# A group's four squared output tiles added on GpSimd before one product with ones, behind the next projection tile

## The reference, cut to what matters

```python
y = y + p['d_skip'][:, None].astype(y.dtype) * xs
y = y.reshape(b, T, D_INNER) * jax.nn.silu(z)
y = rmsnorm(y.reshape(b, T, N_GROUPS, D_INNER // N_GROUPS),
            p['ssd_norm_w'].reshape(N_GROUPS, D_INNER // N_GROUPS)).reshape(b, T, D_INNER)
merged = jax.nn.sigmoid(ga) * (attn @ p['w_pa']) + jax.nn.sigmoid(gb) * (y @ p['w_pb'])
```

## The kernel before, in words

| group | before | later |
|---|---|---|
| 0 | (z, 1, 0) | (z, 1, 1) |
| 1, 2 | (pb, g - 1, 6), two tiles | (z, g + 1, 0), (z, g + 1, 1) |
| 3 | (pb, 2, 6), two tiles | none |

## Time and profile before

### The profile page before, as it was taken

The page is one execution under the profiler, slowest core; times in us unless marked ns, Lnnn a source line. Parts: engine busy times, 40 slices in busy tenths (PEclk is TensorE's granted clock), DMA queues, the critical chain, the costliest instruction groups (busy, mean ns, idle before and its releaser), DMA issues.

```text
span 1709.2 us, 27847 instructions
## 1 busy us (share of the span) xinstructions
PE 1621.0 (95%) x10961; PEld 1453.3 (85%) x10965; DVE 760.9 (45%) x927; ACT 630.9 (37%) x1009; POOL 374.4 (22%) x417
## 2 busy tenths in 40 slices
PE   4998999999999999999999989899989999999997
PEld 3993336888999898889988988899979999999997
DVE  3444454222225667665766665535233333232221
ACT  4437665333223434523533442323132332332221
POOL 6003334542002444344134234100000000000000
PEclk9998999989999999999999999899979999999999
DMA  3221002433332222222223222253202222223331
GB/s 101 80 69 37 0 1 81 136 116 103 96 110 66 86 82 68 87 81 85 68 78 87 81 75 87 64 148 110 63 25 87 85 75 86 86 74 92 102 91 54
DMA packets 189231, 136.74 MB, mean 80 GB/s; under 512 B 7896, under 2 KB 180080, under 8 KB 189087
## 3 DMA queue, kind: packets, MB, share of 16 engines
q1 hardware_dynamic: 177698, 100.02, 20.4%
q0 software_dynamic: 11056, 35.08, 6.8%
q10 hardware_dynamic: 384, 0.37, 0.1%
HBM read 119.78 MB, written 15.67 MB: 79 GB/s over the span
## 4 chain that ended last, share of the span: by engine, by line
PE 51%; DVE 4%; ACT 2%; DMA 1%; issue 1%; POOL 0%; ACTq 0%; POOLq 0%; DVEq 0%
PE tile_banks L378 14%; PE tile_banks L379 14%; PE tile_banks L382 14%; PE spare_bank L1124 2%; PE spare_bank L1116 1%; PE spare_bank L1061 1%; PE spare_bank L1107 1%; PE spare_bank L1096 1%; PE tile_banks L1201 1%; DMA gated_in<-gated_dram 1%; PE spare_bank L1069 1%; PE spare_bank L1089 1%; DVE y_t L1951 1%; DVE w_lo L352 0%; PE spare_bank L1189 0%
## 5 line engine op out<-in xcount | busy, mean ns | idle before, releaser
L378 PE MATMUL tile_banks<-x_hi,w_hi 128*128 128x288 f32 (+1 forms) x1808 | 518.4, 301 | 18.8 <-DVE w_lo L352 10.9
L379 PE MATMUL tile_banks<-x_lo,w_hi 128*128 128x288 f32 (+1 forms) x1808 | 511.9, 298 | 0.0
L382 PE MATMUL tile_banks<-x_hi,w_lo 128*128 128x288 f32 (+1 forms) x1808 | 392.1, 299 | 0.0
L378 PEld LDWEIGHTS tile_banks<-x_hi,w_hi 128*128 128x128 f32 (+1 forms) x1808 | 345.8, 191 | 27.0 <-issue 10.9
L379 PEld LDWEIGHTS tile_banks<-x_lo,w_hi 128*128 128x128 f32 (+1 forms) x1808 | 346.2, 191 | 1.6
L352 DVE TENSOR_TENSOR w_lo<-w_raw,w_hi 128x1024 fp32r<-128x1024 f32 (+2 forms) x169 | 222.4, 1316 | 270.4 <-ACT w_hi L346 268.4
L382 PEld LDWEIGHTS tile_banks<-x_hi,w_lo 128*128 128x128 f32 (+1 forms) x1808 | 294.3, 191 | 0.4
L346 ACT ACTIVATE w_hi<-w_raw 128x1024 fp32r<-128x1024 f32 (+2 forms) x169 | 175.6, 1039 | 120.1 <-PE tile_banks L382 120.0
L800 POOL DMA_DIRECT2D out_y_prompt<-y_tok x8 | 6.3, 786 | 513.5 <-ACT y_tok L1630 513.5
L379 PE MATMUL tile_banks<-f_lo,w_hi 128*128 128x288 f32 x352 | 98.1, 295 | 0.0
L378 PE MATMUL tile_banks<-f_hi,w_hi 128*128 128x288 f32 x352 | 97.9, 294 | 0.0
(11 more groups left out here) (310 smaller groups left out, 2790.3 us busy)
## 6 DMA issues: line engine op xcount, KB each, us to landing
w_raw<-in_w_in SPq DMA_DIRECT2D x68, 512.0 KB, 3.7
w_raw<-in_w_gate SPq DMA_DIRECT2D x22, 512.0 KB, 3.7
w_raw<-in_w_up SPq DMA_DIRECT2D x22, 512.0 KB, 3.6
k_page<-in_cache_k SPq DMA_DIRECT2D x64, 128.0 KB, 2.2
old<-in_state_ssm POOLq DMA_DIRECT2D x32, 256.0 KB, 3.5
out_ssm_sample<-old POOLq DMA_DIRECT2D x32, 256.0 KB, 2.8
w_raw<-in_w_pb SPq DMA_DIRECT2D x16, 512.0 KB, 3.4
w_raw<-in_w_down SPq DMA_DIRECT2D x16, 512.0 KB, 3.9
```

The costliest lines, as they stand in the source:

```text
L378: nc.tensor.matmul(out, wh, xh[:, HALVES[h]], start=start and k == 0, stop=False, skip_group_check=onto)
L379: nc.tensor.matmul(out, wh, xl[:, HALVES[h]], start=False, stop=False, skip_group_check=onto)
L382: mm = nc.tensor.matmul(out, wl, xh[:, HALVES[h]], start=False, stop=stop and k == last, skip_group_check=onto)
```

## The change

The four squares are no longer all multiplied by ones. ScalarE writes square 0 to conv_acc[0] and squares 1, 2, 3 to conv_acc[1]; GpSimd adds conv_acc[1] onto conv_acc[0] three times (`squares_added`), and squares 2 and 3 wait for the add before them. TensorE then does one product for each half. It does so behind the first tile of "later"; in group 3, where there is none, behind the transposes of the convolution tails, which move ahead of it on TensorE, on ScalarE and in `keys`. The orders of slot() on ScalarE and VectorE stay as they are.

```diff
-            keys += [("state_out", g), ("y_ss", g, 0), ("y_ss", g, 1)]
+            keys += [("state_out", g)]
             keys += [("conv_out", j) for j in range(6)] if g == NG - 1 else []
+            keys += [("y_ss", g, 0), ("y_ss", g, 1)]
...
                 eng.dma_start(ssm_prompt[0, 0, g * HG:(g + 1) * HG].rearrange("(j e) p n -> (e p) j n", e=2), state_out[:, :, :]).then_inc(sem("stored_prompt_state"), 16)
+                for j in range(1, PG):
+                    eng.wait_ge(sem("y_squared"), PG * g + j + 1)
+                    if j > 1:
+                        eng.wait_ge(sem("squares_added"), (PG - 1) * g + j - 1)
+                    eng.tensor_tensor(conv_acc[:, 0, 0:T], conv_acc[:, 0, 0:T], conv_acc[:, 1, 0:T], ALU.add).then_inc(sem("squares_added"), 1)
...
+            def turn_tails():
+
+                pe.wait_ge(sem("conv_tails"), CT)
+                for j in range(6):
+                    key = ("conv_out", j)
+                    wait_read(pe, key)
+                    for n in range(4):
+                        mm = pe.transpose(spare(key)[0:27, n * P:(n + 1) * P], conv_out[:, 4 * j + n, :], ident[:, :])
+                    mm.then_inc(bank_full[use[key][0]], 1)
...
-                for key in before:
+                for key in before + later[0:1]:
                     gemm(key)
-
-                for j in range(PG):
-                    pe.wait_ge(sem("y_squared"), PG * g + j + 1)
-                    for h in range(2):
-                        key = ("y_ss", g, h)
-                        if j == 0:
-                            wait_read(pe, key)
-                        mm = pe.matmul(spare(key)[:, 0:HALF], ones[:, :], conv_acc[:, j % 2, HALVES[h]], start=j == 0, stop=j == PG - 1, skip_group_check=True)
-                        if j == PG - 1:
-                            mm.then_inc(bank_full[use[key][0]], 1)
-                    if j < 2:
-                        mm.then_inc(sem("y_summed"), 1)
-                for key in later:
+                if g == NG - 1:
+                    turn_tails()
+                pe.wait_ge(sem("squares_added"), (PG - 1) * (g + 1))
+                for h in range(2):
+                    key = ("y_ss", g, h)
+                    wait_read(pe, key)
+                    pe.matmul(spare(key)[:, 0:HALF], ones[:, :], conv_acc[:, 0, HALVES[h]]).then_inc(bank_full[use[key][0]], 1)
+                for key in later[1:]:
                     gemm(key)
...
                     if j >= 2:
-                        eng.wait_ge(sem("y_summed"), 2 * g + j - 1)
-                    eng.activation(conv_acc[:, j % 2, 0:T], y_t[:, j, :], ACT.Square).then_inc(sem("y_squared"), 1)
+                        eng.wait_ge(sem("squares_added"), (PG - 1) * g + j - 1)
+                    eng.activation(conv_acc[:, min(j, 1), 0:T], y_t[:, j, :], ACT.Square).then_inc(sem("y_squared"), 1)
                     if j == 1:
                         for key in before:
                             slot(key)
+                if g == NG - 1:
+                    for j in range(6):
+                        key = ("conv_out", j)
+                        wait_full(eng, key)
+                        eng.activation(conv_rows[j], spare(key)[0:27, :], ACT.Copy).then_inc(bank_read[use[key][0]], 1)
                 eng.preload_act_table_set("natural_log_exp_and_others")
```

More of the change, by code:

```diff
@@ L1151, in _ @@
                 mm.then_inc(bank_full[use[key][0]], 1)
-                for key in before:
+                for key in before + later[0:1]:
                     gemm(key)
-                for j in range(PG):
-                    pe.wait_ge(sem("y_squared"), PG * g + j + 1)
-                    for h in range(2):
-                        key = ("y_ss", g, h)
-                        if j == 0:
-                            wait_read(pe, key)
-                        mm = pe.matmul(spare(key)[:, 0:HALF], ones[:, :], conv_acc[:, j % 2, HALVES[h]], start=j == 0, stop=j == PG - 1, skip_group_check=True)
-                        if j == PG - 1:
-                            mm.then_inc(bank_full[use[key][0]], 1)
-                    if j < 2:
-                        mm.then_inc(sem("y_summed"), 1)
-                for key in later:
-                    gemm(key)
[L1168 to L1174, removed]
+                if g == NG - 1:
[6 more added lines that the diff above has]
+                for key in later[1:]:
+                    gemm(key)
             for key in last_pb:
@@ L1568, in _ @@
                     slot(key)
[L1569 to L1572, removed]
             for key in last_pb:
```

## The result

The changed kernel is slower: 1752.84 us median (1739.23 to 1755.03, 4 runs) against 1719.09 (1708.73 to 1720.83, 4 runs), ratio 1.0174 with the interval 1.0127 to 1.0222. Measured once more beside the experiments (label e8_after_again), it was 1745.0 against 1718.45, 1.0143 (1.0099 to 1.0186): 26.5 us. The profiled execution of after took 1753.86 us at a span of 1752.4.

A forecast was written before the change was run, and what follows sets the result against it. The prediction took TensorE, busy 95% of the span, to bound the kernel. Shifts 18.5, collision 2.0 and clock 6.7 summed to 27.2 us slower, added to the 1718.95 median for 1746 us, range 1727 to 1754.

The forecast's parts named there:

- The norm chain is exposed in groups 0 to 2: Group ends: the moved z tile no longer covers logarithm-to-split work; TensorE waits 7 us for xdt, 8.3 for w_lo.
- The shifts, 18.5 us: Later start of the logarithm at group ends: 5.5, 6.1, 6.1 and 0.8 us in groups 0 to 3, saved matmuls included.
- the collision, 2.0: GpSimd's first add slows VectorE's weight split for the moved z tile: 0.65 us in each of groups 0 to 2.
- The clock, 6.7 us: Lower granted clock after TensorE's waits: 2.0 us per long wait, less 1.4 already paid in group 1; 0.7 per short one.
- The adds cost nothing on the path: GpSimd's three adds, 1.43 us each in a 5.65 us relay, finish under the z tile with about 3 us of cover.
- Rival 4: GpSimd's adds take 2.5 us or more beside VectorE and end after the z tile: 1751 us, chance 0.06.
- Rival 5, the saving shows: Second z tile's weights split before the products end, nothing exposed, 11.4 us saved: 1707.6 us, chance 0.04.
- The base: Forecast's starting time: the median, 1718.95 us, rather than the profiled span of 1709.2, which lay beside the fastest run.

The follow-up runs named there:

- e8_after_again: The changed kernel itself, unaltered, measured once more beside the experiments: 1745.0 us, 1.0143 of the kernel before.
- e2: The kernel before, with its eight products put behind the first z tile and no adds on GpSimd: 1755.91 us, 1.0198 of the kernel before.
- e3: The changed kernel, with the weight split for the second tile of "later" made ahead of the norm: 1728.16 us, 1.0044 of the kernel before.
- e6: The kernel before, with the change in groups 1 and 2 alone and the second z tile's split ahead of the logarithm: 1716.16 us, 0.9985.
- e5_filled: The changed kernel with matmuls that nobody reads laid into its four long waits: 1743.17 us, 1.0132 of the kernel before.
- e7_filled_again: The changed kernel with its four long waits filled by unread matmuls, measured again beside the changed kernel: 1752.4 us, 1.0155 of the kernel before.

## Why the prediction was right

It forecast 1746 in 1727 to 1754; 1752.84 and 1745.0 were measured. The path and the waits were right in place and length. The term for the clock was not, and that the number fits so well is partly luck. By its steps:

- *The norm chain is exposed in groups 0 to 2.* Shown, by the waits of after at the places and lengths foretold (7.08 us for xdt where 7 were named, 8.21 and 8.22 for w_lo where 8.3, 8.66 ahead of last_pb where 8.7), and by experiment from two sides: e2 has the loss with the place alone, and in e3, with the split put first, most of it is gone.
- *The shifts, 18.5 us, and the collision, 2.0.* The group ends up to the logarithm grew by 25.9. Of that 5.2 are the low clock in the moved tiles (7.98, 7.64 and 9.18 us for three of 6.54). The remaining 20.7 are the 20.5 of the two terms; group 3's share was 1.2, foretold 0.8. The collision alone is 0.6 to 0.7 a group (2.9 against 3.5 and 3.6), foretold 0.65. Over the whole kernel TensorE's idle time grew by 35.8 us in after and by 28.9 in e8_after_again; the forecast's two terms, with the 11.4 us of work saved put back, make 31.9.
- *The clock, 6.7 us.* Too low, and wrongly split. At the changed places it came to about 8: 5.2 behind the three short waits, where 2.1 was charged (1.1 to 2.6 each, where 0.7 was), and 2.8 behind the long ones, where 4.6 was (1.0 in group 0 and 2.0 in group 2 where 2.0 each was, 0.2 less than before in group 1, nothing new ahead of last_pb). Two errors nearly cancel there. Over the whole kernel TensorE's busy time should have fallen by the 11.4 us saved; it rose by 7.4 in after and by 0.7 in e8_after_again (1621.7 against 1621.0). By these sums the clock took some 19 and 12 us more than in the trace of before. How much of this the change brings, and how much is that execution's, stays open; the filling of the long waits shows no gain from a higher clock.
- *The adds cost nothing on the path.* Shown: 1.41 to 1.52 us each against 1.43 estimated (one of 1.82 in group 3), ready 4.5 us or more before the product in groups 0 to 2 and 1.5 in group 3, and no wait for them. Rival 4 is out.
- *Rival 5, the saving shows.* Its condition was the split ahead of y_hi and y_lo. e6 gives it that in the groups that have a second tile, and the kernel is even with before, not faster. The rival left out the 3.5 us ahead of the moved tile, the 1.8 to 1.9 for xdt behind the second, and the lower clock.
- *The base.* The forecast added its change to the median, although the profile's span lay at the lowest run. Over all runs of before here (1706.68 to 1732.98) the median stays at 1717 to 1719, so that was right. The forecast had no reason for the distance of its span from the median; these runs show one: the time goes with the mean granted clock, as with 1706.93 us at 0.960 and 1731.62 us at 0.944.

## What to carry to other kernels

A product that ends a sum is worth moving back only if what waits for the sum is covered by something behind the product; list what stands behind it in every queue, since a weight split at the queue's end made TensorE wait 8.2 us in each of two groups, and the eight saved products were worth 2.85. Look first for waits that the order in a queue alone makes: two instructions moved ahead of y_lo gave 0.4% where the rewritten sum lost 1.4 to 1.7%.

## What was not expected of the hardware

Low clock followed the waits of 2.8 to 3.6 us ahead of the moved tiles of after, not only the waits of 7 to 9 us: 0.79 in group 0, and 0.80 and 0.66 in the windows below for groups 1 and 2.

```profile
841.32:848.60 7.28, 7.28 (x46) 7.28 (x47) 0.52 (x1) 1.97 (x2) 1.86 (x2) 0.80 0.27 73
...
1001.89:1010.80 8.91, 8.91 (x46) 8.91 (x47) 0.52 (x1) 1.97 (x2) 2.06 (x2) 0.66 0.22 61
```

The length of the wait does not settle it. The moved tile of group 0 ran at full clock in e3_after_split_first, behind 2.72 us, and at 0.79 in e8_after_again, behind 2.60 us, with the same instructions ahead of it:

```profile
683.49:690.03 6.54, 6.54 (x49) 6.54 (x50) 0.00 (x0) 1.97 (x2) 2.66 (x2) 1.00 0.30 83
...
691.38:699.35 7.97, 7.97 (x49) 7.97 (x50) 0.00 (x0) 1.97 (x2) 2.63 (x2) 0.79 0.24 68
```

And a higher clock behind the long waits did not show in the time: over their runs TensorE's mean clock was 0.941 to 0.952 in e5_filled and 0.936 to 0.954 in e7_filled_again, against 0.932 to 0.943 in after and 0.939 to 0.950 in e8_after_again, with no gain that the intervals show.
